# Two Transformer blocks on one core: local attention's columns ahead of the third part of the convolution

## The reference

```
h = rms_norm(x, norm1_g);  proj = h @ w_in        # w_in: 1024 x 6912
qa, ka, va, hy_in, qc, kc, vc, gates = split(proj, 512|128|128|1536|512|512|512|3072)
a) local attention: norms and rotary on qa (8 heads of 64), ka (2 heads);
   keys within 128 tokens, softmax with a sink
b) Hyena: u = short_conv(hy_in) (3 taps);  v, x1, x2 = split(u)
   z = x1 * (fft_conv(v, f0) + d0*v);  z = x2 * (fft_conv(z, f1) + d1*z)
c) differential attention with qc, kc, vc: softmax_1 - lam * softmax_2
x = x + (sum over branches of sigmoid(gate) * branch @ w_o) @ w_out;  then an FFN
```

## Time and profile before

| | |
|---|---|
| three plain runs | 1113.09, 1113.66, 1119.86 us (median 1113.66) |
| the profiled execution | 1115.49 us |
| its span, first to last instruction | 1113.7 us |
| instructions | 14635 |
| mean granted clock of TensorE | 0.993 of full |
| moved by DMA | 182.04 MB, mean 163 GB/s |
| stage C in it | from about 643 us on; local heads from about 747 to 818 us |

### The profile page before, as it was taken

How to read it: one execution, slowest core, us unless ns; L and a number is a source line. 1 busy time by engine, 2 the same in 40 slices (tenths; PEclk the granted TensorE clock), 3 DMA queues, 4 the chain that set the end, 5 groups by cost and what they waited for, 6 DMA issues and landing times.

```text
span 1113.7 us, 14635 instructions
## 1 busy us (share of the span) xinstructions
PE 1072.1 (96%) x4942; PEld 865.8 (78%) x4942; DVE 722.5 (65%) x1209; ACT 539.7 (48%) x828; POOL 40.0 (4%) x48
## 2 busy tenths in 40 slices
PE   5999999999999999999999999899999999999998
PEld 3777678888887778788888878676777777888887
DVE  2865876555557987754554579787868666555553
ACT  3564355443444546643443464446456445443442
POOL 5003000000000200000000000000000000000000
PEclk9999999999999999999999999999999999999999
DMA  9464256655565544566555553543444355655553
GB/s 256 123 169 132 77 153 193 191 188 183 189 189 170 169 151 126 158 189 186 189 188 181 179 170 97 168 132 114 136 146 133 118 182 163 190 188 182 189 188 112
DMA packets 133598, 182.04 MB, mean 163 GB/s; under 512 B 11446, under 2 KB 80322, under 8 KB 133490
## 3 DMA queue, kind: packets, MB, share of 16 engines
q1 hardware_dynamic: 132266, 178.40, 50.9%
q0 software_dynamic: 1056, 2.57, 1.1%
q10 hardware_dynamic: 232, 0.49, 0.1%
HBM read 180.36 MB, written 1.05 MB: 163 GB/s over the span
## 4 chain that ended last, share of the span: by engine, by line
PE 76%; DVE 14%; ACT 5%; issue 2%; DMA 1%; SPq 1%; POOL 0%; DVEq 0%; ACTq 0%; POOLq 0%
PE ps L1802 15%; PE ps L1813 14%; PE ps L1805 14%; PE ps L1823 7%; PE ps L1824 7%; PE ps L1828 7%; DVE wlo L998 4%; PE ps L1787 2%; PE ps L1789 2%; PE ps L1788 2%; PE ps L1893 1%; DMA raw<-in_a_w_in 1%; ACT whi L537 1%; PE ps L1876 1%; PE ps L2015 1%
## 5 line engine op out<-in xcount | busy, mean ns | idle before, releaser
L998 DVE TENSOR_TENSOR wlo<-raw,whi 128x1024 fp32r<-128x1024 f32 x338 | 406.6, 1234 | 145.3 <-ACT whi L537 144.7
L537 ACT ACTIVATE whi<-raw 128x1024 fp32r<-128x1024 f32 x338 | 342.3, 1052 | 117.7 <-DMA raw<-in_ffn_w 27.6
L1802 PE MATMUL ps<-whi,ath 128*128 128x512 f32 (+1 forms) x896 | 359.3, 402 | 8.3 <-DVE atl L1012 4.3
L1805 PE MATMUL ps<-whi,atl 128*128 128x512 f32 (+1 forms) x896 | 351.4, 393 | 0.0
L1813 PE MATMUL ps<-wlo,ath 128*128 128x512 f32 (+1 forms) x896 | 241.4, 391 | 3.3 <-DVE wlo L998 3.3
L1802 PEld LDWEIGHTS ps<-whi,ath 128*128 128x128 f32 x896 | 169.6, 189 | 52.6 <-issue 12.0
L1813 PEld LDWEIGHTS ps<-wlo,ath 128*128 128x128 f32 x896 | 168.0, 189 | 40.3 <-DVE wlo L998 5.3
L1805 PEld LDWEIGHTS ps<-whi,atl 128*128 128x128 f32 x896 | 169.8, 189 | 33.3 <-issue 0.5
L1823 PE MATMUL ps<-whi,brh 128*128 128x512 f32 x272 | 106.5, 392 | 0.4 <-issue 0.4
L1824 PE MATMUL ps<-whi,brl 128*128 128x512 f32 x272 | 105.9, 389 | 0.0
L1074 DVE TENSOR_TENSOR brl<-ps,brh 128x512 fp32r<-128x512 f32 x33 | 22.8, 692 | 94.6 <-ACT brh L583 94.6
(11 more groups left out here) (339 smaller groups left out, 1006.5 us busy)
## 6 DMA issues: line engine op xcount, KB each, us to landing
raw<-in_ffn_w_in SPq DMA_DIRECT2D x176, 256.0 KB, 2.9
raw<-in_ffn_w SPq DMA_DIRECT2D x132, 256.0 KB, 2.9
raw<-in_w_in SPq DMA_DIRECT2D x104, 256.0 KB, 2.9
raw<-in_ffn_w_out SPq DMA_DIRECT2D x88, 256.0 KB, 2.8
raw<-in_a_w_in SPq DMA_DIRECT2D x48, 256.0 KB, 3.3
raw<-in_b_w_in SPq DMA_DIRECT2D x48, 256.0 KB, 3.0
raw<-in_a_w_out SPq DMA_DIRECT2D x16, 256.0 KB, 2.8
raw<-in_b_w_out SPq DMA_DIRECT2D x16, 256.0 KB, 2.8
```

Of the source, the lines that this page charges most:

```text
L537: a_(unit_view(whi, slot, w), unit_view(raw, slot, w), ACT.Copy).then_inc(hi_ready, 1)
L998: v_.tensor_tensor(unit_view(wlo, slot, w), unit_view(raw, slot, w), unit_view(whi, slot, w), ALU.subtract).then_inc(lo_ready, 1)
L1802: mm(ps[bk + t][:, 0:w], ath[:, k, t * P:(t + 1) * P], rh[:, kk, :], start=k == 0, stop=False)
L1805: mm(ps[bk + t][:, 0:w], atl[:, k, t * P:(t + 1) * P], rh[:, kk, :], start=False, stop=False)
```

## The change

The order of the columns: blocks 14 and 15 are now local q and local k and v (256 columns), block 16 the third part of the convolution. The widths follow (units U_C+12 to 15 are narrow, not U_C+16 to 19). TensorE's steps of the convolution stand between other units of these blocks. ScalarE evacuates 14, takes 15 and the local squares ahead of `h_back(1)`, and evacuates the third part behind `h_odd(1)`. VectorE does the local sums, the norms and the turning of tile 0's eight q heads between `hyena_gate(0)` and `spectral(1)`; the rest of the turning stays where it was. ScalarE issues one extra exponential of a single column ahead of its wait for the turned q and k. In the heads' loop the first head's exponential goes ahead of the feed, its `w_prob(0)` into step 0, `obh` into step 0, the squares for differential attention to the end of step 1, and the feed of step 8 behind `w_pt(7)` on ScalarE and out of the loop (to the feed behind it) on VectorE.

```diff
-C_COLS = ((768, 512), (1280, 512), (1792, 512), (0, 512), (512, 256), (2304, 512), (2816, 512), (3328, 512))
+C_COLS = ((768, 512), (1280, 512), (0, 512), (512, 256), (1792, 512), (2304, 512), (2816, 512), (3328, 512))
+H_BLOCKS = (12, 13, 16)
         def unit_width(u):
-            return 256 if U_C + 16 <= u < U_C + 20 else 512
+            return 256 if U_C + 12 <= u < U_C + 16 else 512
...
@@ ScalarE
             h_conv(1)
-            h_evac(2)
-            feed(U_C + 19)
+            evac(14, lambda t: C_pa[:, t, 0:512], n=4, tiles=(0, 1))
             feed(U_C + 18)
-            h_back(1)
-            feed(U_C + 19)
-            h_odd(1)
-            feed(U_C + 20)
-            evac(15, lambda t: C_pa[:, t, 0:512], n=4, tiles=(0, 1))
-            feed(U_C + 23)
-            evac(16, lambda t: C_pa[:, t, 512:768], n=4, tiles=(0, 1))
-            act.wait_ge(evac_act, ACT_EVACS[16])
+            evac(15, lambda t: C_pa[:, t, 512:768], n=4, tiles=(0, 1))
+            act.wait_ge(evac_act, ACT_EVACS[15])
             c_squares([(C_z[:, 0:640], C_pa[:, 0, 0:640]), (hid_flat, C_pa[:, 1, 0:512]),
                        (sil_flat[:, 0:128], C_pa[:, 1, 512:640])])
-            feed(U_C + 24)
-            act.wait_ge(sem("h_prod"), 10)
+            feed(U_C + 19)
+            h_back(1)
+            feed(U_C + 21)
+            h_odd(1)
+            feed(U_C + 22)
+            h_evac(2)
+            feed(U_C + 23)
             h_conv(2)
             feed(U_C + 27)
             evac(17, lambda t: C_pd[:, t, 0:512], n=4, tiles=(0, 1))
             feed(U_C + 30)
+
+            a_(sm[:, 126:127], con[:, 0:1], ACT.Exp)
             act.wait_ge(sem("c_w_turned"), 1)
...
             feed(U_C + 32)
-            act.wait_ge(sem("h_z"), 4)
-            a_(obh[:, :, :], h_v, ACT.Copy).then_inc(sem("h_hi"), 1)
             evac(18, lambda t: C_pd[:, t, 512:1024], n=4, tiles=(0, 1))
...
             for i in range(WQ + 2):
-                if i == 1:
-                    act.wait_ge(evac_act, ACT_EVACS[18])
-                    c_squares(...)
...
-                feed(W_STEPS[min(i, WQ)])
+                if i == 0:
+                    w_exp(0)
                 if i < WQ:
+                    feed(W_STEPS[i])
+                if 0 < i < WQ:
                     w_exp(i)
+                if i == 0:
+                    act.wait_ge(sem("h_z"), 4)
+                    a_(obh[:, :, :], h_v, ACT.Copy).then_inc(sem("h_hi"), 1)
                 if 0 <= i - 1 < WQ:
                     w_pt(i - 1)
+                if i == WQ:
+                    feed(W_STEPS[WQ])
+                if i == 1:
+                    act.wait_ge(evac_act, ACT_EVACS[18])
+                    c_squares(...)
...
@@ VectorE
             hyena_gate(0)
-            feed(U_C + 20)
-            spectral(1)
-            feed(U_C + 21)
-            spectral_imag(1)
-            feed(U_C + 22)
-            spectral_end(1)
-            feed(U_C + 24)
+            feed(U_C + 18)
+
             c_sums(0, C_z[:, 0:640], 300, 10)
             c_sums(1, hid_flat, 310, 8)
             c_sums(2, sil_flat[:, 0:128], 318, 2)
+            c_norms(3, 300, 20)
+            limit[0] = U_C + 19
+            link(c_rotate(0, 0, 8, 0, None))
+            feed(U_C + 20)
+            spectral(1)
+            feed(U_C + 22)
+            spectral_imag(1)
+            feed(U_C + 24)
+            spectral_end(1)
+            feed(U_C + 25)
             h_taps(2)
             feed(U_C + 26)
             limit[0] = U_C + 30
-            c_norms(3, 300, 20)
             for t in range(NT):
-                link(c_rotate(t, 0, 8, 0, None))
-                tick()
+                if t:
+                    link(c_rotate(t, 0, 8, 0, None))
+                    tick()
                 link(c_rotate(t, 512, 2, 1, None))
...
             hyena_gate(1)
-            feed(U_C + 32)
+            feed(U_C + 31)
...
             for i in range(WQ + 2):
-                if 0 <= i - 1 < WQ:
+                if 1 <= i - 1 < WQ:
                     w_prob(i - 1)
                 if i < WQ:
                     w_logits(i)
+                if i == 0:
+                    feed(U_C + 32)
+                    w_prob(0)
...
-                feed(W_STEPS[min(i, WQ)])
+                if i < WQ:
+                    feed(W_STEPS[i])
...
@@ TensorE
             units(14, 0, 3)
             h_turn(1)
             units(14, 3, 4)
-            units(15, 0, 1)
+            units(15, 0, 2)
             backward(0)
-            units(15, 1, 3)
+            units(15, 2, 4)
+            units(16, 0, 1)
             h_back(1)
-            units(15, 3, 4)
+            units(16, 1, 2)
             forward(1)
-            units(16)
+            units(16, 2, 4)
             units(17, 0, 1)
             h_turn(2)
             units(17, 1, 4)
```

More of the change, by code:

```diff
@@ L799, in h_evac @@
             def h_evac(c):
-                evac(12 + c, lambda t: C_ph[:, c, t, :], n=4, tiles=(0, 1))
+                evac(H_BLOCKS[c], lambda t: C_ph[:, c, t, :], n=4, tiles=(0, 1))
             def h_conv(c):
@@ L897, in _ @@
                 if i == 1:
-                    act.wait_ge(evac_act, ACT_EVACS[18])
-                    c_squares([(C_z, C_pd[:, 0, 0:1024]), (hid_flat, C_pd[:, 1, 0:512]),
-                               (sil_flat, C_pd[:, 1, 512:1024])])
-                if i == 1:
                     evac(19, lambda t: C_pd[:, t, 1024:1536], n=4, tiles=(0, 1))
@@ L908, in _ @@
                     gate_evac(22, 0)
-                feed(W_STEPS[min(i, WQ)])
+                if i == 0:
+                    w_exp(0)
                 if i < WQ:
+                    feed(W_STEPS[i])
+                if 0 < i < WQ:
                     w_exp(i)
+                if i == 0:
+                    act.wait_ge(sem("h_z"), 4)
+                    a_(obh[:, :, :], h_v, ACT.Copy).then_inc(sem("h_hi"), 1)
                 if 0 <= i - 1 < WQ:
                     w_pt(i - 1)
+                if i == WQ:
+                    feed(W_STEPS[WQ])
+                if i == 1:
+                    act.wait_ge(evac_act, ACT_EVACS[18])
+                    c_squares([(C_z, C_pd[:, 0, 0:1024]), (hid_flat, C_pd[:, 1, 0:512]),
+                               (sil_flat, C_pd[:, 1, 512:1024])])
                 if i >= 3 and i % 2 == 1:
@@ L2233, in h_turn @@
             def h_turn(c):
-                pe.wait_ge(evac_act, ACT_EVACS[12 + c])
+                pe.wait_ge(evac_act, ACT_EVACS[H_BLOCKS[c]])
                 if c:
```

## The result

The changed kernel took 1105.89 us (median of 5, 1103.83 to 1107.89) where the kernel before took 1113.66 in the same set. The ratio of their means is 0.9909, 95% interval 0.9883 to 0.9934, which is 10.1 us less (7.4 to 13.0). A second set beside the experiments gave 0.9928 (0.9913 to 0.9943), 8.0 us less (6.3 to 9.7). Median against median the first set gives 7.8 us. The forecast was 1104.3, a gain of 9.4. Two executions stand far apart from all others and are in no ratio: 1795.78 us for the kernel before, at 0.558 of the full clock, and 6127.10 us for the changed kernel in the second set, at full clock. The profiled execution took 1104.78 us with a span of 1103.0, 10.7 under the span before.

A forecast was written before the change was run, and what follows sets the result against it. TensorE, 96% busy, was taken as the bound. Holes and clock losses of 10.5 us, less one left, gave 10.4, less 0.4 for ties 10.0; 9.4 was taken for the median: 1104.3 us, range 1101.5 to 1108.5.

The forecast's parts named there:

- TensorE as the bound, holes as the only prize: Whole kernel: TensorE is busy in 96% of the span, so a change of order can win no more than holes.
- The layout of the new order: Stage C up to the second head: each engine followed with old durations, bringing p_turn(1) to 754.5 instead of 764.92.
- The ties: Unit 24's low half and the gate's sums arrive just when wanted, each late by 0 to 0.4 us; 0.4 taken off.
- So 6.3 us of work went before it at no cost.: VectorE before spectral(1): sums, norms and tile 0's turning fit into its 7.13 us hole, adding 6.3 us of work free.
- The first clock term: TensorE from 719.01 to 724.37, behind the 2.73 us hole: 1.7 us lost to the clock and the restart.
- The sum of 10.5: TensorE's stage C up to the second head: idle, hidden idle, clock and restart losses total 10.5 us, all the change can find.
- One of the two in my sum isn't theirs: Plain runs' median, 1.8 us below the profiled execution, may have one clock loss fewer; 9.4 us taken for the median.
- The extra Exp: ScalarE before the first head: one-column exponential pulls the 1.28 us table load into idle time, not changing the sum.
- A: Convolution, before unit 24: VectorE is late by 2 to 3 us and the clock loss stays; gain 5 to 6, chance 0.15.
- B: Hole at 894.54: its slow clock, 1.6 us, goes and ties are won, giving 1101.7 to 1102.3; chance 0.15.
- C: Convolution's second half: VectorE becomes the bound and the kernel slower, 1118 at 25% longer steps; chance 0.03.
- Rival D: VectorE's sums and norms start only after h_back(1), so only the heads' beginning is won: 4.4 us, 1109.3; chance 0.07.

The follow-up runs named there:

- e5: The changed kernel run and profiled again with no edit: median 1106.83 us, ratio to the kernel before 0.9928.
- e4: The changed kernel with sums, norms and tile 0's turning put back behind spectral_end(1), new column order kept: 1114.68 us, ratio to before 0.9997.
- e7: The changed kernel with one extra VectorE product (0.73 us) before spectral(1): 75.99 us from h_turn(1) to the second head's turn.
- e8: The changed kernel with four extra VectorE products (2.9 us) before spectral(1): 78.13 us from h_turn(1) to the second head's turn.
- e10: The kernel before, unedited, in a third profile: 84.24 us from h_turn(1) to the second head's turn.
- e11: The kernel with norms and turning late but new column order, repeated without edit: 82.79 us from h_turn(1) to the second head's turn.
- e6: The changed kernel with block 24's evacuation ahead of d_exp(2) and half the last merge ahead of a feed: 1102.47 us, ratio to before 0.9884.
- e3: The changed kernel without the extra one-column exponential: 75.70 us from h_turn(1) to the second head's turn.
- e1: The kernel before with only the heads' part of the change, including the extra exponential: 1111.87 us, ratio to before 0.9972.
- e9: The kernel before, unedited, in a second profile: 85.70 us from h_turn(1) to the second head's turn.
- e2: The changed kernel with the heads' part undone, so the convolution's part alone: 1109.5 us, ratio to before 0.9955.

## Why the prediction was right, point by point

**TensorE as the bound, holes as the only prize.** Right. e5 repeats D to 0.01, and the parts add.

**The layout of the new order.** Taken from 1.11 us later, as this execution began, nearly every instant came as laid out: `h_turn(2)` 711.3 forecast, 711.23 measured; spectral(1) 703.9 and 703.95; the turns 737.6 and 737.50; p_turn(0) 748.3 and 748.30; p_turn(1) 755.6 and 755.61. The one idle time of VectorE, for unit 23, was forecast at 0.55 and was 0.28: VectorE came there 0.1 later than laid out and ScalarE's split 0.1 earlier, and the rest is the end of a drawn row. The ties cost 0.0 and not the 0.4 that I took off.

**"So 6.3 us of work went before it at no cost."** Right and the larger half: e4 shows what the same column order is worth without it, 6.9 us of D. The 6.9 include one slow clock. The cover was there; behind it VectorE has some 0.35 us left in front of unit 20 (e7, e8), where the layout had 0.4.

**The first clock term was priced wrongly.** "From 719.01 to 724.37 are 5.36 us for four matmuls and a unit: 1.7 lost to the clock and the restart" counted a loss and put it beside holes as if it would go by itself. e10 shows the kernel before with a full clock in that place and the same arrival, by a hole of 1.18. The sum of 10.5 was nonetheless right for that profile, because hole and slow clock stood for the same missing `wlo`. What it was not right for is other executions: the gain is 84.24 or 85.83 less 75.4, so 8.8 or 10.4, by whether the second slow clock comes.

**From the profile to the median.** "One of the two in my sum isn't theirs" was the right doubt, but it took both for equal: only the second comes and goes at a price. Two profiles with full clock in D and tail bear that out: the span of e10 is 8.8 us over that of e5, and 84.24 less 75.42 is 8.8. I took 9.4 off the median without a sum for the last 0.6, and it lies between the sets' 10.1 and 8.0; the median came out at 1105.89, 1.6 over the forecast. That it is so near is in part luck, since single executions scatter by more than their D: TensorE's `h_turn(1)` began anywhere from 679.1 to 684.2 us in the thirteen profiles. Part of that is there from the start: the first product that waits for `atl` began at 16.32 us in the first profile, 17.02 in the changed one, 20.43 in e11 and 20.90 in e6.

**The extra Exp.** "Neither changes my sum" held (0.3 us), though by the way of the evacuation and with the load running ahead of the wait, as told under 3.

**The rivals.** A needs a delay that isn't there (e7, e8). B came true in the profiled pair: the slow clock behind the hole near 894 is missing in the changed kernel's profile although the hole (2.23 us) is there. It shows in the tails: 348.78 against 347.39, so 1.39 and not 1.6, which with 10.42 and the late start of 1.11 makes the 10.70 of the spans. e3 had it again at 885.6, e8 near 888. C did not happen. Rival D is refuted by the sums' start at 695.22, ahead of `h_back(1)`'s end.

## What to carry to other kernels

When one engine is 96% busy, list its waits, take each back to the engine that was late, and look for the idle time which that engine had a little earlier: work moved into it costs nothing as long as the next wait still comes out in time, and here the old rows gave that slack to within a tenth or two of a us. Waits of that kind sit in the order of an engine's own queue and can be bought one by one; the same reading of two more waits gave another 4 us (e6). In this kernel a slow clock was lost time only where TensorE, and not the engine that feeds it, set the arrival.

## What the runs showed that I had not expected

- A slow clock of TensorE behind a hole may cost nothing: 63.04 us to the turns with it and without it (first profile and e10).
- A hole of the same length has a slow clock behind it or not: 2.7 us with it (first profile of before, e1, e9) and without (e10), the first head's 1.7 us with (first profile, e2, e9) and without (e10), 2.2 us near 890 with (first profile, e3, e4, e8) and without (eight others); behind the 2.42 us in e8 there was none.
- A table load starts before the wait of the exponential that needs it is met (e3: 743.53, exponential at 744.83), so with 1.08 us of idle at that place it costs 0.3 of D and not 1.28.
